# Moving the activation splits, the mixer outputs and the weight ring to other byte offsets in SBUF

## What is computed

```python
h = h + 0.5 * swiglu(rmsnorm(h, ffn1_norm[i]), ffn1_w_gate[i], ffn1_w_up[i], ffn1_w_down[i])  # 1024 -> 2816 -> 1024
u = rmsnorm(h, mix_norm[i]) @ w_in[i]
y = concat([y_mla(u), y_mlstm(u), y_fnet(u)])      # attention, mLSTM scan, 2-D DFT
h = h + y @ w_out[i]
h = h + 0.5 * swiglu(rmsnorm(h, ffn2_norm[i]), ...)
h = h + sigmoid(rmsnorm(h, ple_gate_norm[i]) @ ple_w_gate[i]) * rmsnorm(p[i] @ ple_w_proj[i], ...)
```

## Time and profile before

| | |
|---|---|
| median of 3 runs | 3914.24 us |
| span of the profiled execution | 3897.8 us |
| what the median has beyond that span | 16.4 us |
| TensorE busy with matmuls | 3723.0 us, 96% |
| TensorE busy with weight loads | 2868.5 us, 74% |
| VectorE / ScalarE / GpSimd busy | 2205.6 / 1298.2 / 722.5 us |
| mean granted TensorE clock | 0.963 |
| moved by DMA | 345.43 MB, mean 89 GB/s |

### The profile page before, as it was taken

One profiled execution on the slowest core, in us unless ns is written; L12 is line 12 of the kernel. 1 busy time (PEld: TensorE's weight loads), 2 busy tenths in 40 slices (PEclk: granted clock), 3 DMA queues, 4 the chain that ended last, 5 costly groups with the idle time before them and its releaser, 6 DMA issues. The chain is left out here.

```text
span 3897.8 us, 42134 instructions
## 1 busy us (share of the span) xinstructions
PE 3723.0 (96%) x16630; PEld 2868.5 (74%) x16630; DVE 2205.6 (57%) x2994; ACT 1298.2 (33%) x1873; POOL 722.5 (19%) x434
## 2 busy tenths in 40 slices
PE   8999998999999999998999989888999999989999
PEld 6888734888878888635888876685888766867887
DVE  6545556655565455457645576765444657745443
ACT  3222235522242223335422344445222343443221
POOL 3432002343213430001434013020000020200000
PEclk9999998999999999999999999798999998989999
DMA  4443200343324342102343221001222220012222
GB/s 170 140 138 104 96 18 27 135 139 130 120 93 133 129 136 87 60 23 86 133 138 133 92 79 60 6 1 65 92 93 102 78 75 21 1 49 83 96 98 81
DMA packets 92947, 345.43 MB, mean 89 GB/s; under 512 B 10832, under 2 KB 11088, under 8 KB 91856
## 3 DMA queue, kind: packets, MB, share of 16 engines
q1 hardware_dynamic: 92752, 342.74, 26.3%
HBM read 340.60 MB, written 2.10 MB: 88 GB/s over the span
## 5 line engine op out<-in xcount | busy, mean ns | idle before, releaser
L381 ACT ACTIVATE w_hi<-raw 128x1024 fp32r<-128x1024 f32 (+2 forms) x540 | 561.0, 1040 | 1927.2 <-PE ps L325 1912.4
L323 PE MATMUL ps<-xs_hi,w_hi 128*128 128x512 f32 x2472 | 982.0, 397 | 34.9 <-DVE xs_lo L542 16.2
L324 PE MATMUL ps<-xs_lo,w_hi 128*128 128x512 f32 x2472 | 971.3, 393 | 0.0
L325 PE MATMUL ps<-xs_hi,w_lo 128*128 128x512 f32 x2472 | 970.3, 393 | 0.0
L391 DVE TENSOR_TENSOR w_lo<-raw,w_hi 128x1024 fp32r<-128x1024 f32 (+2 forms) x540 | 669.8, 1241 | 126.1 <-ACT w_hi L381 125.9
L323 PEld LDWEIGHTS ps<-xs_hi,w_hi 128*128 128x128 f32 x2472 | 469.1, 190 | 160.3 <-issue 33.7
L325 PEld LDWEIGHTS ps<-xs_hi,w_lo 128*128 128x128 f32 x2472 | 469.4, 190 | 99.6
L324 PEld LDWEIGHTS ps<-xs_lo,w_hi 128*128 128x128 f32 x2472 | 469.8, 190 | 98.7 <-issue 3.6
L323 PE MATMUL ps<-hd_hi,w_hi 128*128 128x512 f32 x1320 | 527.6, 400 | 3.5 <-DVE hd_lo L484 3.5
L324 PE MATMUL ps<-hd_lo,w_hi 128*128 128x512 f32 x1320 | 524.7, 398 | 0.0
L325 PE MATMUL ps<-hd_hi,w_lo 128*128 128x512 f32 x1320 | 524.2, 397 | 0.0
(11 more groups left out here) (454 smaller groups left out, 4316.7 us busy)
## 6 DMA issues: line engine op xcount, KB each, us to landing
raw<-in_ffn_gu SPq DMA_DIRECT2D x264, 512.0 KB, 3.7
arena<-in_ada SPq DMA_DIRECT2D x64, 768.0 KB, 5.6
raw<-in_ffn_dn SPq DMA_DIRECT2D x96, 448.0 KB, 3.3
raw<-in_in_t SPq DMA_DIRECT2D x60, 512.0 KB, 3.6
raw<-in_ffn_dn SPq DMA_DIRECT2D x48, 512.0 KB, 3.5
raw<-in_out SPq DMA_DIRECT2D x32, 512.0 KB, 3.6
raw<-in_pleg SPq DMA_DIRECT2D x16, 512.0 KB, 3.5
raw<-in_in_r SPq DMA_DIRECT2D x8, 512.0 KB, 3.8
```

What stands on the lines that cost most here:

```text
L323: T.matmul(bank, lhs_hi(k), rhs_hi(k), start=(first and k == 0), stop=False)
L324: T.matmul(bank, lhs_hi(k), rhs_lo(k), start=False, stop=False)
L325: mm = T.matmul(bank, lhs_lo(k), rhs_hi(k), start=False, stop=(last and k == kt - 1))
L381: A.activation(self.hi[:, n % HL, 0:size], raw[:, n % RAW, 0:size], ACT.Copy).then_inc(self.high_done, 1)
```

## The change

It changes where tensors lie, and no instruction. `mod` is no longer a tensor but another name for `ada`, so `modulation` writes its sum over its input, and 384 bytes a partition are saved. The arena begins at the next multiple of 128 bytes (before: of 32). `REST` grows from 13064 to 13088 words, so `xs` begins at a multiple of 128 bytes too. 16 words (64 bytes) are left free ahead of the weight ring.

```diff
-    mod = sb("mod", [P, DEPTH, 48])
     gain2 = sb("gain2", [P, DEPTH, 16])
     ada = sb("ada", [P, DEPTH, 48])
+    mod = ada
...
-    REST = 13064
-    SPARE = 1810
+    REST = 13088
+    SPARE = 1808
+    LINE = 128
     HD_AT, REST_AT = 0, SPLIT
     X_AT = SPLIT + REST
-    HL_AT = X_AT + SPLIT
+    HALF_LINE = 16
+    HL_AT = X_AT + SPLIT + HALF_LINE
     SPARE_AT = HL_AT + 2 * HL * CW
     WORDS = SPARE_AT + SPARE
-    fence_at = -(-nc.sbuf_base // 32) * 32
-    fence = sb("fence", [P, WORDS + 8])
+    fence_at = -(-nc.sbuf_base // LINE) * LINE
+    fence = sb("fence", [P, WORDS + (fence_at - nc.sbuf_base) // 4])
+    assert all(4 * at % LINE == 0 for at in (HD_AT, REST_AT, X_AT))
```

## The result

The changed kernel takes 3936.49 us (median of 4 runs, 3932.46 to 3939.08) against 3913.42 us: 1.0065 times the kernel before, with a 95% interval of 1.0053 to 1.0077. It is 23 us slower where 31 us less were forecast. The profiled span grew from 3897.8 to 3934.1 us. That is 36 us and not 23.

A forecast was written before the change was run, and what follows sets the result against it. TensorE was taken as the bound, its matmul step times their number; 32.3 us saved on hd and ys, 0 for xs, 1 us given back made -31 us, from 3914.2 to 3883 us; 8-in-10 range 3750 to 3893.

The forecast's parts named there:

- part (1): hd and ys move from 32 to 0 past 128: 4824 products fall from 233.3 to 226.6 ns, saving 32.3 us.
- (5): Shorter hd products leave less time to hide VectorE's work, and half-clock products gain nothing: 1 us given back.
- part (2): xs moves from 64 to 0 past 128, ring stays at 64: 7704 products, taken to cost 0.
- The slower one: Split products pay for the distance between operands' offsets, 6.7 ns per 32 bytes: up to 4049 us; chance 13%.
- Its point of decision: The slower rival decides the sign once xs loses over 4.2 ns a product (32.3 us / 7704).
- The larger gain: Unit is 128 bytes, so an operand at 64 also pays: split products save 116 to 161 us, 3798 to 3753; chance 32%.
- The 215.8 ns: Skill's step for a 512-column matmul, 10.8 ns under the trace's 226.6; if all products reached it, about -167 us.
- Parts costed at nothing: VectorE's writes to the moved splits and its sum written over ada: 0 each, the sum below 1 us at worst.

The follow-up runs named there:

- a_zero: Kernel before with mod = ada and 224 bytes left free ahead of xs, so xs, hd, ys and ring start equal modulo 256; 3878.39 us, ratio 0.9918.
- a_shift: Kernel before with mod = ada and the whole arena moved, all distances between operands kept; 3911.0 us, ratio 1.0002.
- c_line256: Changed kernel with LINE = 256, REST = 13120, HALF_LINE = 0: xs, hd, ys, ring at multiples of 256 bytes; 3877.93 us, 0.9908 times the kernel before.

## Why the prediction was wrong, point by point

**The bound was right.** TensorE sets the pace, the number of steps is right, and a gain in the step reaches the end: a_zero gave 31 us (3909.2 to 3878.4, medians of the same series), the sum that part (1) and (5) had for a fall of `hd` and `ys` from 233.3 to 226.6. VectorE and the DMA took nothing noticeable back.

**The step that failed** is "the simplest reading of the rows is that an operand must begin at a multiple of 64 bytes", and with it part (2), "by the boundary of 64 bytes it costs 0". It mistook a distance between two operands for a property of each. The rows before had 0, 32 and 224 as the only distances, and every pair with a 32 in it was also a pair at unequal offsets, so the two readings could not be told apart there. Part (1) then measured 4.3 ns in place of 6.7, because `hd` went to distance 64, not 0; part (2) measured +48 us in place of 0. Offsets modulo 128 were too coarse as well: worked out modulo 256, the same addresses in the front part put `hd` at 64 and `xs` at 192 from the ring after the change.

**The rivals.** The slower one had the right variable, though modulo 128, and the wrong law. Its "64 for every pair" is 64 for `hd` and `ys` and 192 for `xs`. It let the price grow by 6.7 ns for each 32 bytes, up to 4049 us; in fact the price is one step, 5.6 to 7.7 ns for any distance but 0 (and about 2.3 at 64), so `xs` lost 6.4 ns and `hd` still gained. Its point of decision held: `xs` passed 4.2 ns a product (3.1 ns with the 24 us that `hd` and `ys` really gained). The argument against it, "a price for distance should show in the plain products too, and they are flat", could not be made from those rows. By the buffers of the kernel, both operands of L1605 come from one region at equal remainders modulo 256, and so do both of L1773: both rows are at distance 0. The trace of the kernel before does have plain products at other distances, 224 and 32 (`uq` or `ukv` with the normed `cq` or `ckv`, right behind the input projection):

```profile
485.49 25.05 PE L315 MATMUL ps<-arena 128*128 128x512 f32 x58
```

Less one record of 0.592 us over 57 steps that is 429.1 ns, no dearer than the 429.7 of the earlier trace rows, which are at distance 0. So plain products don't pay, as the prediction said, but that says nothing about fp32r products, which take their columns at twice the pace and do pay. The larger gain assumed a price for an operand at 64 by itself; a_shift and a_zero exclude that. The slower rival had a chance of 13% but no place in the range: its upper end of 3893 lies below the kernel before, and the time fell above both, at 3936.

**The rules of the Trainium skill.** Between the kernel before and a_zero the pace of the `hd` products changes with where their two operands lie to each other, from 233.3 to 226.8 ns. The Trainium skill, SBUF — State Buffer, section "Who interferes with whom", gives the tensor engine independent read ports and lets it wait on nobody. By that rule a distance could not matter; the traces disagree for fp32r products at full clock, and using the rule against the distance rival would have been a mistake. Whether it is at the read ports that the two meet, no run shows. No kind of product of 512 columns came below 226.5 ns on average. The 215.8 ns that the prediction took from the Trainium skill, TensorE: Matmul & The Clock Gate, section "Back-to-back issue gap", are given there for a single matmul and not for a stream, and no placement reached them.

**Parts costed at nothing.** `mod = ada` and the moved writes were indeed free (a_shift; VectorE's L979 into `hd_lo` has the median of 693 ns of the earlier trace rows in the kernel after too). At the half clock nothing is paid after the change either. Six steps of `xs` at distance 192 take 2.56 us, 427 ns each, as in the earlier trace rows:

```profile
2398.93 0.63 PE L327 MATMUL ps<-xs_lo,w_hi 128*128 128x512 f32 x1
...
2401.49 0.63 PE L327 MATMUL ps<-xs_lo,w_hi 128*128 128x512 f32 x1
```

## What to carry to other kernels

In an fp32r kernel that TensorE bounds, put the moving and the stationary operands at the same remainder modulo 256 bytes, all of them and both halves of a split; which remainder it is didn't matter in the placements tried. Here, with nearly all products 512 columns wide, it was worth 0.8% (a_zero) and 0.9% (c_line256) with no instruction changed. It is shown for this one kernel at the full clock. When a trace shows a few nanoseconds between kinds of one instruction, list the start addresses of every operand and look at differences and at moduli larger than the first that fits, and if two readings fit the rows, ask which of the pairs after the change neither has covered.

## What was not expected of the hardware

- The pace of an fp32r product of 512 columns at 2.4 GHz depends on the distance of its operands modulo 256 bytes: 226.7 ns at 0, 229 at 64, 232.3 to 234.4 at the other six multiples of 32. Over 213.3 ns that is 32, 38 and 46 to 51 column times. Products of 384 columns pay 2 ns at 128 and nothing at 64, and plain float32 products nothing at 32 or 224.
- A single displaced operand among the four of a group (`w_lo` by 32 bytes) makes the three products pay 6.7 ns on average, +73 us in all against a_zero. The kernel before, with `hd` and `ys` wholly displaced, is 31 us over a_zero.
- Reading the stationary operand with step 0 doesn't bring a product to the cheap pace: 231.6 and 231.0 ns, against 226.7 for a full tile at distance 0.
- At 1.2 GHz none of this is to be seen: 427 ns, 512 columns and nothing more.
